# First head pair's decay factors moved into the value projection, its chunk loop moved next with gate matmuls and page sums inside

## What is computed

```python
h = rmsnorm(x, norm1)
z = h @ w_in                      # gq 256 | gk 256 | gv 512 | gr 512 | g_lr 16 | dq 512 | dk 512 | dv 512
log_a = log_sigmoid(g_lr @ w_a2 + b_a) / 16
# gated heads: S_t = diag(exp(log_a_t)) S_{t-1} + k_t^T v_t, o_t = q_t S_t, in exact chunked form
gla_o = rmsnorm(gla_o, gla_g) * silu(gr)
# differential attention: prompt over itself, samples over 1024 cached keys in pages of 128
diff_o = softmax(q1 k1) v - lam * softmax(q2 k2) v
x = x + concat(gla_o, rmsnorm(diff_o)) @ w_out
x = x + hier_moe(rmsnorm(x, norm2), ...)
```

## Time and profile before

| | us |
|---|---|
| median of 3 runs (lowest, highest) | 904.08 (902.46, 907.13) |
| the profiled execution | 903.2 |
| its span, first to last instruction | 901.4 |
| PE busy in the span | 781.4 (87%) |
| DVE busy | 567.9 (63%) |
| ACT busy | 443.8 (49%) |
| POOL busy | 244.6 (27%) |

### The profile page before, as it was taken

One profiled execution on the slowest core, in us unless ns is written; L12 is line 12 of the kernel. 1 busy time (PEld: TensorE's weight loads), 2 busy tenths in 40 slices (PEclk: granted clock), 3 DMA queues, 4 the chain that ended last, 5 costly groups with the idle time before them and its releaser, 6 DMA issues. The chain is left out here.

```text
span 901.4 us, 16428 instructions
## 1 busy us (share of the span) xinstructions
PE 781.4 (87%) x6255; PEld 493.1 (55%) x6255; DVE 567.9 (63%) x922; ACT 443.8 (49%) x854; POOL 244.6 (27%) x170
## 2 busy tenths in 40 slices
PE   4999979869899999987899999975279999998784
PEld 3666634335456653434456666533178787776541
DVE  6643559677354452138787777345948677787848
ACT  6432012366763321226458676534317767777733
POOL 3112977730225000002001000100522543442204
PEclk9999989989999999997999999997579999999998
DMA  9415785701013258893111111147486889999864
GB/s 315 103 51 152 232 288 156 247 0 48 1 46 102 81 174 251 261 302 127 47 71 54 66 71 47 51 157 246 130 269 199 299 275 301 319 342 340 247 210 188
DMA packets 98691, 154.70 MB, mean 172 GB/s; under 512 B 13573, under 2 KB 63301, under 8 KB 98610
## 3 DMA queue, kind: packets, MB, share of 16 engines
q1 hardware_dynamic: 91266, 132.97, 44.5%
q0 software_dynamic: 5728, 16.94, 7.5%
q10 hardware_dynamic: 1616, 3.70, 1.1%
...
## 5 line engine op out<-in xcount | busy, mean ns | idle before, releaser
L922 POOL TENSOR_TENSOR kv<-kv,gt 128x1024 f32<-128x1024 f32 x32 | 80.6, 2544 | 52.8 <-DMA kv<-in_cache_k 52.6
L2378 PE MATMUL ps<-hT_reg,w_reg 128*128 128x344 f16 x280 | 86.6, 309 | 0.0
L2379 PE MATMUL ps<-hT_reg,w_reg 128*128 128x344 f16 x280 | 86.5, 309 | 0.0
L2380 PE MATMUL ps<-hT_reg,w_reg 128*128 128x344 f16 x280 | 86.5, 309 | 0.0
L950 POOL TENSOR_TENSOR rst<-rst,neghalf 128x1 f32<-128x1 f32 (+3 forms) x27 | 24.7, 917 | 215.3 <-DVE rst L1892 215.3
L2378 PE MATMUL ps<-w_reg,hT_reg 128*128 128x512 f16 x192 | 73.7, 384 | 1.9 <-ACT kv L1171 1.9
L990 POOL DMA_INDIRECT sum_scratch<-kv,dest x23 | 52.4, 2279 | 83.8 <-DMA sum_scratch<-kv,dest 77.5
L2379 PE MATMUL ps<-w_reg,hT_reg 128*128 128x512 f16 x192 | 73.5, 383 | 0.0
L2380 PE MATMUL ps<-w_reg,hT_reg 128*128 128x512 f16 x192 | 73.3, 382 | 0.0
L1911 DVE TENSOR_REDUCE mxs<-ps 128x1 f32<-128x640 f32 (+7 forms) x48 | 45.7, 952 | 30.0 <-PE ps L2751 29.8
L1636 DVE TENSOR_REDUCE gbc<-kv 128x16 f32<-128x1024 f32 x32 | 38.8, 1214 | 27.2 <-POOL kv L922 27.1
...
## 6 DMA issues: line engine op xcount, KB each, us to landing
...
```

What stands on the lines that cost most here:

```text
L922: pool.tensor_tensor(pg, pg, qbc[:, b % 2].unsqueeze(1).to_broadcast([P, 2, 512]), ALU.mult).then_inc(s_kq, 1)
L2378: pe.matmul(out, lh, rh, start=start, stop=False)
L2379: pe.matmul(out, lh, rl, start=False, stop=False)
L2380: return pe.matmul(out, ll, rh, start=False, stop=stop)
```

## The change

1. **Buffers.** `ek` and `ed` move from weight slot 0 to staging buffer 1, `ea` to the memory of `es`, `eb` and the second pair's softplus to that of `code`. Weight halves 7 to 10 and 12 all go through staging buffer 0, half 11 through buffer 1 (table `STAGE`).
2. **First pair's decays inside GV.** ACT no longer waits for all GV matmuls; shifts, query decays, key decays and the rest stand between its reads of GV tiles 3, 5 and 7, and the second pair's softplus comes before the loop and no longer in it.
3. **PE order.** After GV comes one quarter of GR tile 0 (six matmuls), then loop 0 with one more quarter after the transpose of each of the chunks 0 to 6. So GR tiles 0 and 1 are made in the loop.
4. **DVE order.** The read of CODE goes ahead of page sums 11 and 12. Sums 21 to 31, the maxima, the second pair's `log_decay` and all its running sums are in loop 0, after the state update of a chunk.
5. **Weight loads and splits.** SP issues halves 7, 8 and 9 ahead of page steps 10, 18 and 25 (before: 17, 19 and 26, and half 10 at 28), half 10 after the pages. The first DKG half is split on ACT in loop 0 (chunk 3) and on DVE ahead of the second pair's products, the second one after loop 1.
6. **Gate reads and samples.** `gate_read(0)` is at loop 0's chunk 7, `gate_read(1)` after the loop, `gate_read(3)` between key decays and `ed`. The maxima's reduction over partitions is ahead of POOL's gate steps; the samples' exponentials and sums go from loop 0 to loop 1.

```diff
+STAGE = [0, 1, 0, 1, 0, 1, 0, 0, 0, 0, 0, 1, 0]
...
-        o = 2 * 2048
-        ek = w_reg[:, o:o + 1024]
-        ed = w_reg[:, o + 1024:o + 2048]
-        ea = w_reg[:, o + 2048:o + 3072]
-        eb = w_reg[:, o + 3072:o + 3584]
-        softplus1 = w_reg[:, o + 2048:o + 2048 + T]
+        ek = stage[1][:, 0:1024]
+        ed = stage[1][:, 1024:2048]
...
+        ea = es[:, 0:SEQ]
...
+        eb = code[:, 0:SEQ // 2]
+        softplus1 = code
...
-            late = {17: HALVES_TO[GV], 19: HALVES_TO[GV] + 1, 26: HALVES_TO[GR], 28: HALVES_TO[GR] + 1}
+            late = {10: HALVES_TO[GV], 18: HALVES_TO[GV] + 1, 25: HALVES_TO[GR]}
...
+            plain_read(gv_even[1])
+            shifts(0)
+            act.wait_ge(s_z, 6)
+            query_decays()
+            plain_read(gv_even[2])
+            act.wait_ge(s_wl, STAGE_BEFORE[HALVES_TO[DKG]] + 1)
+            key_decays()
+            chunk_decays(0)
+            softplus(1)
+            read_parts(GV)
+            plain_read(gv_even[3])
...
-                if p == 0:
-                    act.wait_ge(s_mm, UNITS_TO[GV])
...
-                    if p == 0 and c == 1:
-                        act.wait_ge(s_prep, 1)
-                        softplus(1)
+                    if p == 0 and c == 3:
+                        split_w(HALVES_TO[GR])
+                    if p == 0 and c == 7:
+                        gate_read(0)
...
+                    if p == 0 and c < NT:
+                        if c == 0:
+                            log_decay(1)
+                        for n in ((), (21, 22), (23,), (24, 25), (26,), (27, 28), (29,), (30, 31))[c]:
+                            page_scores(n)
+                        if c == NT - 1:
+                            page_maxima()
...
+                    if p == 0 and c < NT:
+                        running_sums(1, range(c, c + 1))
...
+            def gate_quarter(t, q):
+                u = UNIT_AT[(GR, t, 0)]
+                sh, sl = slot_h[SLOT[GR]], slot_l[SLOT[GR]]
+                if q == 0:
+                    pe.wait_ge(s_wl, HALVES_TO[GR])
+                    pe.wait_ge(s_ev[BANK[u]], NTH[u] - 1)
+                for k in range(2 * q, 2 * q + 2):
+                    ins = split_mm(ps[:, BANK[u], :], hTh[:, k, span(t)], hTl[:, k, span(t)], sh[:, k, :], sl[:, k, :],
+                                   k == 0, k == KC - 1)
+                if q == 3:
+                    ins.then_inc(s_mm, 1)
...
-                project(GR, only=(range(0, 2), range(2, 6))[p])
+                if p:
+                    project(GR, only=range(2, 6))
                 if p == 0:
+                    gate_quarter(0, 0)
...
+                        if p == 0 and c < NT - 1:
+                            gate_quarter((c + 1) // 4, (c + 1) % 4)
```

148 lines of the change are left out of this document (76 added, 72 removed).

## The result

The changed kernel takes 898.09 us (median of 20 runs, 893.55 to 902.20) against 906.38 us of the kernel before (20 runs, 901.70 to 910.50) measured beside it: a ratio of 0.9914, with a 95% interval of 0.9898 to 0.9930. It is faster by 0.86%, some 7.8 us. The forecast was 889 us, nearly 15 us under the 904.08 us known then; its sign held and its size did not, though the time lies inside the range of 882 to 899.

A forecast was written before the change was run, and what follows sets the result against it. PE, busy for 781.4 of 901.4 us, was taken as the bound. 167.5 + 32.3 + 24.4 + 21.9 = 246.1 us against 260.95, 14.9 us less, gave 889.2 us; range 882 to 899 (0.83).

The forecast's parts named there:

- Part 1: Up to loop 0: the chain over DVE and ACT starts loop 0 at 167.5 us instead of 193.0, bounds 163.5 to 170.
- PE's wait of 4.56 us and its slow products go: Ahead of loop 0: DVE reads the code at about 114 us instead of 124, ending PE's wait and slow code products.
- Part 2: Loop 0 with seven gate quarters and the added DVE work takes 32.3 us, bounds 30 and 37; before 24.0.
- rival C: Loop 0: small PE gaps drop the clock to 1.2 GHz, loop some 28 us longer, kernel 917 us; chance 0.04.
- Part 3: From loop 0's end to loop 1's start: 24.4 us with waits for gate reads, bounds 22.8 and 26; before 22.75.
- Part 4: Loop 1 and behind: samples' exponentials and sums move into loop 1, 21.2 becomes 21.9 us, bounds 21.2 and 22.5.
- I take it to shift as a whole: The program behind loop 1 is nearly unchanged, so the 14.9 us won by then carry to the end.
- rival L: From the experiments, no chance given: time won earlier is given back in the experts' stage, where the DMA share is 1.0.
- A: DVE and pages bound loop 0: it takes 37 to 42 us, kernel 896 to 902 us; chance 0.10.
- B: All covers hold: POOL stalls between page sums 20 and 21, DVE products run quietly, 881 to 883 us; chance 0.08.
- D: Decays do not move ahead of GV's end, loop 0 starts near 180, kernel 899 to 903 us; chance 0.03.

The follow-up runs named there:

- e10: The changed kernel itself run again on another chip: 896.83 us, ratio 0.9939 to the kernel before.
- e4: Changed kernel with POOL's reductions of the maxima and sums moved behind gate steps 3 and 5: 892.76 us, ratio 0.9875 to the kernel before.
- e8: The kernel of e4 run again on another chip with five rounds: 887.54 us, ratio 0.9813 to the kernel before.
- e5: e4 with page sum 10 on DVE moved behind its reads of the gated query/key tiles and code: 892.93 us, ratio 0.9871 to the kernel before.
- e1: Changed kernel with POOL's reduction of the maxima back behind gate step 1: 896.44 us, ratio 0.9910 to the kernel before.
- e11: The kernel of e4 run again, beside the changed kernel on one chip: 890.20 us, ratio 0.9858 to the kernel before.
- e2: Changed kernel with the reduction of the maxima replaced by a plain POOL copy (samples' results wrong): 889.08 us, ratio 0.9857 to the kernel before.
- e6: Changed kernel with the reduction of the maxima made twice in a row: 898.22 us in a single run.
- e7: Changed kernel with all eight gate quarters ahead of loop 0 and none in it: 904.10 us, ratio 1.0015 to the kernel before.
- e12: Changed kernel with a small TENSOR_TENSOR and a second reduction added behind the reduction of the maxima: 910.88 us, ratio 1.0090 to the kernel before.

## Why the prediction was right in sign and wrong in size

**Part 1, loop 0's start (167.5; measured 169.1) held, but not all its reasons.** "PE's wait of 4.56 us and its slow products go" was half right. The products have their 1.90 us, but a new wait of 3.16 us stands earlier, ahead of GV tile 0, and the code products start at 125.33 us, not near 120 (121.68 in e10, the same kernel). I had followed the weight half that is loaded at page step 10 to DVE's split, and not to the pages queued behind it on SP's queue. POOL and DVE in the changed kernel:

```profile
113.22 15.98 POOL L926 TENSOR_TENSOR kv<-kv,gt 128x1024 f32<-128x1024 f32 x6 [3.71 <-DMA kv<-in_cache_k]
```

```profile
115.63 1.22 DVE L1665 TENSOR_REDUCE gbc<-kv 128x16 f32<-128x1024 f32 x1 [4.86 <-POOL kv L926]
116.77 0.50 DVE L1637 TENSOR_SCALAR dg_reg<-ps 128x344 f32<-128x344 f32 x1
```

The page product waits for its transfer, page sum 10 waits for the product, and the tile read that PE needs stands behind that sum. That the page was late because of the weight half ahead of it is read from the order of SP's queue (the half is issued at 104.41 us, the next pages from 105.60); no run moves the half itself. The wait was between nothing of note and 3.16 us in the kernels that share this stretch (2.27 in e4, 2.00 in e8), and e5 shows that taking it away does not start loop 0 earlier: the chain over DVE and ACT to the sample tile sets the start, as Part 1 has it. In the changed kernel's own trace the two ends meet: ACT's read ends at 166.23 us, and PE, busy without a gap since 117.42, reaches the sample tile at 166.87. The chain's point of 144.5 us for the running sums was measured at 145.8 in e8 and 148.3 in the changed kernel. Single traces spread more than Part 1's bounds (163.5 to 170) allow: with this stretch the same, loop 0 starts between 164.9 (e1) and 171.9 us (e11), at 166.6 in e10.

**Part 2, the length of loop 0 (32.3; measured 32.9), held.** The clock stayed at 1.00 between 170 and 200 us with waits of up to 1.69 us, so rival C, which needs a low clock for half the loop, is refuted. But the clock did fall at the loop's end: 0.87 from 200 to 202 us, behind the wait of 2.15 us, and 0.50 from 202 to 204, for a loss of 1.6 us that the sum did not have. In e8 the window of 190 to 200 us, with a wait of 1.67 us in it, has 0.66; in e10, with waits of 1.55 and 1.51 us, it did not fall at all. Of the fall and rise that the Trainium skill tells of (TensorE: Matmul & The Clock Gate, "A second HAM failure mode: psum-queue depth-cycling") the eleven traces of this loop show one in five of them (the changed kernel, e1, e2, e6, e8), in the last two chunks or right behind them, and none in the other six. DVE was busy for 9.72 of the ten us from 190. Two chunks in the loop, one with POOL quiet and one beside its page products (182.04 to 189.27 us), tell apart the operations that POOL slows. DVE in the changed kernel, a scan, two masks, and then two page sums, a scan and two masks:

```profile
178.34 0.41 DVE L1713 TENSOR_TENSOR_SCAN mix_reg<-ones,mix_reg 128x128 f32<-128x128 f32 x1
178.77 0.42 DVE L1783 TENSOR_TENSOR gs_reg<-ps,mask_ji 64x256 f32<-64x256 f32 x1
179.20 0.29 DVE L1785 TENSOR_TENSOR gs_reg<-ps,mask_ji 64x128 f32<-64x128 f32 x1
...
183.40 2.35 DVE L1665 TENSOR_REDUCE gbc<-kv 128x16 f32<-128x1024 f32 x2
185.66 1.47 DVE L1713 TENSOR_TENSOR_SCAN mix_reg<-ones,mix_reg 128x128 f32<-128x128 f32 x1
187.14 0.42 DVE L1783 TENSOR_TENSOR gs_reg<-ps,mask_ji 64x256 f32<-64x256 f32 x1
187.57 0.29 DVE L1785 TENSOR_TENSOR gs_reg<-ps,mask_ji 64x128 f32<-64x128 f32 x1
```

```profile
182.04 7.23 POOL L926 TENSOR_TENSOR kv<-kv,gt 128x1024 f32<-128x1024 f32 x3 [18.86 <-DMA kv<-in_cache_k]
```

The scan, with two inputs in SBUF, goes from 0.41 to 1.47 us; the masks, with one in PSUM, stay at 0.42 and 0.29. That is what the rule cited in Part 2 (the Trainium skill, SBUF — State Buffer, "Who interferes with whom") says. Of the eight scans in the loop the three beside a page product took 1.05 to 1.47 us and the five others 0.41 to 0.43, together 5.7 us, in the middle of the 3 to 7.5 that the sum allowed.

**Part 3 is the step that failed.** "POOL adds: its reduction of the maxima, 5.61 + 0.54 us, is now ahead of the gate steps that a gate read waits for, about 1 us of the first wait." The term was mis-sized: POOL's stop was 15.4 us and not 6.15, since it also pays on the way back from the reduction, so the stop no longer hid behind DVE's late tail. It became a wait of 6.19 us, and behind that the clock was low for half a tile (2.5 us lost). The forecast had 3.6 us for all waits of the stretch, about 1 of them for the reduction; the waits and the low clock came to 10.3. The traces without the stop there have 22.5 to 22.9 us for the stretch, those with it 30.7 to 32.0 (e7 apart, whose loop 0 ends later): the term is worth some 8 us, and the forecast's other waits in the stretch (1.5, 1.4 and 0.7 us) were somewhat too long, since without the stop waits and low clock together are 1.7 to 2.1 us. The times agree: without the stop, or with it elsewhere, the ratio is 0.9857 and 0.981 to 0.988, and the forecast is 0.983.

The price could be read before the change. The row that I used (5.61 us ahead of the reduction) shows the way there alone; the way back was hidden there, because the next gate step came only at 226.52 us, after a wait of 22.47 us for ACT. The other reduction of the same kernel, on the sums, has both. POOL in the kernel before:

```profile
244.29 0.73 POOL L939 PARTITION_ALL_REDUCE dmb<-dmx  x1 [5.76 <-issue]
252.12 1.26 POOL L930 TENSOR_TENSOR kv<-kv,gt 128x512 f32<-128x512 f32 x1 [7.11 <-issue]
```

With 5.6 + 0.5 + 7.1 us from these rows, the first gate step starts 13.2 us behind the last page product. The forecast names no time for that product; if it ends near 199.5 us, just ahead of the forecast's end of loop 0, the step's two instructions (2.5 us) and ACT's read of the tile (1.1) end near 216.3, where Part 3 has GR tile 4 start at 199.8 + 10.4 + 1.5 = 211.7. The forecast would have been 4 to 5 us longer, near 893.5, and the clock behind the wait brings it nearer still.

The Trainium skill (GPSIMD Engine Reference, "2.1 Instruction dispatch") says that new code is loaded into the engine at run time, and that the first call behind a load pays about 6 us that no instruction shows. The rows agree for the way there: 5.5 to 6.1 us wherever no other wait covers it. For the way back they show 6.7 to 8.8 us, which that section doesn't give. That code is loaded at each change would fit e12, but no trace shows what is loaded.

**Part 4 (21.9; measured 21.65) held.** "I take it to shift as a whole" held for the changed kernel: 6.2 us less at GR tile 6, 6.9 less at the end. It holds less well for a larger gain. In e8 the samples' transposes start at 255.50 us, 17.5 less than before (273.02), and the span is 11.6 less; in e11 the two are 12.3 and 5.8, in e2 17.7 and 5.6, in e4 15.1 and 10.9. In e8 and e11 most of this goes between 260 and 400 us, where PE waits for the value pages by DMA (3.62 us at 383.18 in e8, 1.45 us at 397.55 before) and, in e11, has a granted clock of 0.67 from 380 to 400. In e2 and e4 a large part goes behind 634 us, in the experts' stage: there they are still 12.4 and 14.8 us ahead. The profiled executions of e8, e11 and e2 were slower than their medians, that of e4 was not (892.31 against 892.76), so a part of a large gain seems to be given back, how much regularly stays open, and rival L is neither shown nor excluded for it.

**The rivals.** A (DVE and the pages bound, 896 to 902) has the measured time, but not by its mechanism: its loop 0 of 37 to 42 us was 32.9 (37.2 in e1 alone). B's stop of POOL came (18.86 us of idle time before 182.04) and its time didn't. D is refuted by loop 0's start. C is refuted as a fall for half the loop, as said above.
